# Second block, second mixer: the attention units begin in the column of the sparse keys, and two turns of results move between the tiles of the last query column

## What is computed

```
def odd_mixer(x, w_in, q_norm_g, kv_norm_g, w_uq, w_ukv, w_o):
    qc, kc, vc, qi, ki, wi, cq, ckv, kr = split_cols(x @ w_in, ODD_SIZES)
    out_c = dsa_attention(qc, kc, vc, qi, ki, wi)      # 8 heads, 64 best keys by an index score
    q  = rms_norm_2(cq, q_norm_g) @ w_uq               # 8 heads of 64 + 32 (rotated)
    kv = rms_norm_2(ckv, kv_norm_g) @ w_ukv            # 8 heads of 64 keys + 64 values
    out_d = causal_block_attention(q, k, v)            # k: kv's keys and the shared rotated kr
    return concatenate([out_c, out_d], axis=-1) @ w_o
```

## Time and profile before

| what | us |
|---|---|
| median of 3 timed runs | 2582.02 |
| lowest and highest of them | 2581.15, 2609.4 |
| the profiled execution, its own time | 2592.51 |
| its span, first to last instruction | 2590.7 |
| busy in the span: PE, DVE, ACT | 2452.1, 1719.2, 1194.5 |
| mean granted PE clock | 0.953 of full speed |

### The profile page before, as it was taken

How to read it: one execution, slowest core, us unless ns; L and a number is a source line. 1 busy time by engine, 2 the same in 40 slices (tenths; PEclk the granted TensorE clock), 3 DMA queues, 4 the chain that set the end, 5 groups by cost and what they waited for, 6 DMA issues and landing times.

```text
span 2590.7 us, 34009 instructions
## 1 busy us (share of the span) xinstructions
PE 2452.1 (95%) x14244; PEld 2102.6 (81%) x14244; DVE 1719.2 (66%) x2263; ACT 1194.5 (46%) x1520; POOL 98.7 (4%) x187
## 2 busy tenths in 40 slices
PE   5999999899999999999999998989999899899998
PEld 1788888767789999998899997867777787778776
DVE  5897776652656656655556655568878775688786
ACT  3222212333434444445444444456656644566665
POOL 0111111010000000000000000000000000000000
PEclk8999999998869999999899998999999896999999
DMA  6677887322114554455334452238877630388774
GB/s 257 216 243 255 267 265 260 131 76 95 66 35 161 179 195 163 175 193 217 139 131 164 178 203 99 82 128 332 333 270 297 252 114 33 114 330 321 287 301 181
DMA packets 80387, 501.19 MB, mean 193 GB/s; under 512 B 9604, under 2 KB 10708, under 8 KB 28496
## 3 DMA queue, kind: packets, MB, share of 16 engines
q1 hardware_dynamic: 59120, 423.66, 44.4%
q0 software_dynamic: 21088, 75.01, 9.1%
HBM read 497.58 MB, written 1.05 MB: 192 GB/s over the span
## 4 chain that ended last, share of the span: by engine, by line
PE 69%; DVE 16%; ACT 9%; issue 3%; DMA 2%; DVEq 0%; ACTq 0%; SPq 0%; POOL 0%; POOLq 0%
PE bank L394 67%; DVE wl L1913 7%; ACT wh L1304 6%; DVE macc L1949 2%; ACT s L1394 1%; DVE f L2074 1%; PE bank L577 1%; DMA raw<-in_wstream 1%; DVE s L2065 1%; DMA raw<-in_wmod 1%; PE bank L1198 1%; DVE rs L1973 1%; DVE hl L2049 1%; ACT H L1403 0%; DVE tmp L2042 0%
## 5 line engine op out<-in xcount | busy, mean ns | idle before, releaser
L1913 DVE TENSOR_TENSOR wl<-raw,wh 128x2048 fp32r<-128x2048 f32 (+1 forms) x430 | 903.8, 2107 | 404.7 <-ACT wh L1304 402.1
L1304 ACT ACTIVATE wh<-raw 128x2048 fp32r<-128x2048 f32 (+1 forms) x430 | 755.0, 1763 | 366.4 <-PE bank L394 354.3
L394 PE MATMUL bank<-hh,wh 128*128 128x258 f32 (+2 forms) x2200 | 700.8, 319 | 43.9 <-DVE wl L1913 23.5
L394 PE MATMUL bank<-hh,wl 128*128 128x258 f32 (+2 forms) x2200 | 681.5, 310 | 0.0
L394 PE MATMUL bank<-hl,wh 128*128 128x258 f32 (+2 forms) x2200 | 680.1, 309 | 0.0
L394 PEld LDWEIGHTS bank<-hh,wh 128*128 128x128 f32 x2200 | 428.1, 195 | 72.3 <-issue 23.0
L394 PEld LDWEIGHTS bank<-hl,wh 128*128 128x128 f32 x2200 | 429.0, 195 | 18.5
L394 PEld LDWEIGHTS bank<-hh,wl 128*128 128x128 f32 x2200 | 427.4, 194 | 19.2
L394 PE MATMUL bank<-wh,hh 128*128 128x512 f32 (+1 forms) x704 | 278.4, 395 | 5.5 <-DVE hl L2825 2.8
L394 PE MATMUL bank<-wl,hh 128*128 128x512 f32 (+1 forms) x704 | 274.0, 389 | 0.0
L394 PE MATMUL bank<-wh,hl 128*128 128x512 f32 (+1 forms) x704 | 274.0, 389 | 0.0
(11 more groups left out here) (424 smaller groups left out, 2716.8 us busy)
## 6 DMA issues: line engine op xcount, KB each, us to landing
raw<-in_wstream SPq DMA_DIRECT2D x393, 1024.0 KB, 5.0
mring<-in_wmod POOLq DMA_DIRECT2D x128, 512.0 KB, 4.6
raw<-in_wmod SPq DMA_DIRECT2D x8, 1024.0 KB, 9.1
X<-in_xT SPq DMA_DIRECT2D x1, 2048.0 KB, 12.3
bias<-in_nabias POOLq DMA_DIRECT2D x16, 128.0 KB, 2.5
c_sglg<-in_sglg POOLq DMA_DIRECT2D x1, 1024.0 KB, 5.2
c_sglb<-in_sglb POOLq DMA_DIRECT2D x1, 1024.0 KB, 7.5
out<-X SPq DMA_DIRECT2D x4, 256.0 KB, 2.2
```

Of the source, the lines that this page charges most:

```text
L394: return e.matmul(out, lhsT, rhs, start=start, stop=stop, skip_group_check=True)
L1304: e.activation(wh[i % NB][:, o], raw[i % NR][:, o], ACT.Copy).then_inc(*slab_high(st.split + m))
L1913: e.tensor_tensor(wl[i % NB][:, o], raw[i % NR][:, o], wh[i % NB][:, o].bitcast(F32), ALU.subtract).then_inc(*slab_low(st.split + m))
```

## The change

The column okc moves from before the latent projections to behind them, and five unit steps go into it, each followed by a selection step. The oqc columns 1 and 2 have six unit steps each where there were five, and column 3 has five. Its turns 2 and 3 stand behind its tiles 5 and 6. So all 22 steps that came before the output projection are now between tiles, and `attend(5)` and the loop of turns and units are gone. `middle` becomes a table from tile to function. ACT copies both turns out, does unit 21 and only then copies out the last oqc column. DVE makes both low parts and then does unit 21. The projection's own 14 steps are as before. Four selection steps of okc are gone, and a later step stands between units for each.

```diff
--- before.py
+++ after.py
@@ -981,7 +980,7 @@
                 ins.then_inc(*result("ossq"))
 
 
-            def p(chunks, c0, key, m0=0, pumps=False, units=(), middle=None):
+            def p(chunks, c0, key, m0=0, pumps=False, units=(), middle={}):
                 for m in range(m0, m0 + chunks):
                     b = bank((key, m), act_out, key, m)
                     st.kept.add(bank_of[key, m])
@@ -993,13 +992,13 @@
                         if k in units:
                             attend(1)
                             pump(1)
-                        if k == 3 and middle:
-                            middle()
+                        if k in middle:
+                            middle[k]()
                     st.kept.remove(bank_of[key, m])
 
             p(2, 8, "ocq")
             p(1, 10, "ock")
-            p(1, 7, "oki", middle=root_sum)
+            p(1, 7, "oki", middle={3: root_sum})
             p(2, 5, "oqi")
             project_tok("oin", 12, P, 2, h, dve_out, "ovw")
             st.selection = selection()
@@ -1012,8 +1011,7 @@
                 w.wait_ge(const_in["oswap"], 0)
                 mm(b[:, 0:n * T].rearrange("p (h t) -> p h t", h=n), od.osw[:], src, True, True).then_inc(*result(*key))
 
-            p(1, 0, "oqc", pumps=True, middle=lambda: rotate(("rot", "kr"), od.kr[:].unsqueeze(1), act_out, "okr", 0))
-            p(1, 4, "okc", pumps=True)
+            p(1, 0, "oqc", pumps=True, middle={3: lambda: rotate(("rot", "kr"), od.kr[:].unsqueeze(1), act_out, "okr", 0)})
 
             def q_part(m):
                 b = bank(("uq", m), act_out, "uq", m)
@@ -1068,14 +1066,15 @@
 
             st.kept.update(range(5))
             st.units = attention("od", OD, od.a, logits, values, (4,))
-            p(3, 0, "oqc", m0=1, units=OD_UNITS)
+            def turn_in(i):
+                turned(i, bank(("turn", "od", i), dve_out, "turn l", "od", i))
+
+            p(1, 4, "okc", units=(1, 2, 4, 5, 7))
+            p(2, 0, "oqc", m0=1, units=(0, 2, 3, 4, 6, 7))
+            p(1, 0, "oqc", m0=3, units=(0, 1, 2, 4, 7), middle={5: lambda: turn_in(2), 6: lambda: turn_in(3)})
             result.mark("h read", "oin")
             pump(100)
             pad()
-            attend(5)
-            for i in (2, 3):
-                turned(i, bank(("turn", "od", i), dve_out, "turn l", "od", i))
-                attend(1)
             out_banks("wo1")
             for d in range(6):
                 for k in (4, 6):
@@ -1750,8 +1749,6 @@
             st.selection = selection()
             p(1, "okr", lambda m: od.kr[:], pumps=True)
             p(1, "oqc", query, 0.125, pumps=True)
-            p(1, "okc", lambda m: od.kc[:], pumps=True)
-
             def q_part(m):
                 taken(2)
                 w.wait_ge(result, "uq", m)
@@ -1772,19 +1769,22 @@
             for q in range(2):
                 e.activation(od.vD[:, q, :], banks[bank_of["ovd", q]][:], ACT.Copy).then_inc(*act_out("ovd", q))
             st.units = attention("od", OD, od.a)
-            p(3, "oqc", query, 0.125, m0=1, units=(2, 3))
-            pump(100)
-            pad()
-            attend(5)
 
             def turned(i):
                 w.wait_ge(result, "turn", "od", i)
                 e.activation(hh[:, 2 * i:2 * i + 2, T:2 * T], banks[bank_of["turn", "od", i]][:].rearrange("p (c t) -> p c t", c=2),
                              ACT.Copy).then_inc(*act_out("turn h", "od", i))
 
-            for i in (2, 3):
-                turned(i)
+            def turns():
+                for i in (2, 3):
+                    turned(i)
                 attend(1)
+                pump(100)
+
+            p(1, "okc", lambda m: od.kc[:], units=(2, 3))
+            p(2, "oqc", query, 0.125, m0=1, units=(3, 3))
+            p(1, "oqc", query, 0.125, m0=3, units=(3, 1), middle=turns)
+            pad()
             for _ in range(14):
                 attend(1)
                 taken(2)
@@ -2678,8 +2678,6 @@
             pump(2)
             rotate(("rot", "kr"), od.kr[:].unsqueeze(1))
             pump(2)
-            taken(KC)
-            pump(4)
             for m in (4, 5, 0, 1, 2, 3):
                 taken(2)
                 if m == 1:
@@ -2703,23 +2701,21 @@
                 e.scalar_tensor_tensor(b[:, 0:n], od.dd[:, qb, 0:n], slope, b[:, 0:n], ALU.mult, ALU.add).then_inc(*dve_out("od biased", u))
 
             st.units = attention("od", OD, od.a, logits, lambda g: heads_of(od.Y, g % 2, 512 if g < 2 else 0))
-            for n in 3 * (2, 3):
+            def turned(i):
+                w.wait_ge(act_out, "turn h", "od", i)
+                e.tensor_tensor(hl[:, 2 * i:2 * i + 2, T:2 * T], banks[bank_of["turn", "od", i]][:].rearrange("p (c t) -> p c t", c=2),
+                                hh[:, 2 * i:2 * i + 2, T:2 * T].bitcast(F32), ALU.subtract).then_inc(*dve_out("turn l", "od", i))
+
+            for n in (2, 3, 3, 3, 3, 3, 3, 1):
                 for _ in range(n):
                     attend(1)
                     pump(1)
                 taken(4)
+            for i in (2, 3):
+                turned(i)
+            attend(1)
             pump(100)
             pad()
-            attend(5)
-
-            def turned(i):
-                w.wait_ge(act_out, "turn h", "od", i)
-                e.tensor_tensor(hl[:, 2 * i:2 * i + 2, T:2 * T], banks[bank_of["turn", "od", i]][:].rearrange("p (c t) -> p c t", c=2),
-                                hh[:, 2 * i:2 * i + 2, T:2 * T].bitcast(F32), ALU.subtract).then_inc(*dve_out("turn l", "od", i))
-
-            for i in (2, 3):
-                turned(i)
-                attend(1)
             for _ in range(14):
                 attend(1)
                 taken(2)
```

More of the change, by code:

```diff
@@ L93 @@
 SELECTION_STEPS = 14
-OD_UNITS = (1, 2, 4, 5, 7)
 W1 = T + 2
```

## The result

| what | before | after |
|---|---|---|
| median of timed runs, us | 2582.02 (17 runs) | 2614.6 (17 runs) |
| lowest and highest | 2574.23, 2620.47 | 2585.95, 2626.01 |
| the profiled execution, its own time | 2592.51 | 2626.01 |
| its span | 2590.7 | 2624.2 |
| mean granted PE clock | 0.953 | 0.939 |

The ratio of after to before is 1.0098, with a 95% interval of 1.0067 to 1.0129. It is the ratio of the means without the slow runs (one of before's and two of after's): 2612.2 against 2586.8 us, 25.4 us apart, where the medians are 32.6 apart, since before's runs spread upwards. The change costs about 1% (17 to 33 us by the interval). That lies within the 2% of the forecast's chances, but it is clear of no change. The profiled execution of after is the highest of its 17 runs.

A forecast was written before the change was run, and what follows sets the result against it. TensorE, busy 95% of the span, and its clock bound the kernel. From 2115.9, 72.6 us at 0.50 plus a 1.2 us wait reach 2189.7 against 2161.61: +28 on 2582.0, forecast 2610 us; own range 2600 to 2617, wider range 2576 to 2618.

The forecast's parts named there:

- PE ends the value projection at 2109: Before okc: moving okc's tiles and four score matmuls away ends PE's value projection at about 2109, not 2115.0.
- DVE gains only a split, PE is freed at 2115.9 after 1.8 us: Start of okc: DVE saves one 0.60 us split; PE waits 1.8 us for unit 0's exponential, to 2115.9.
- The clock falls between 2113 and 2118: Inside okc: too few wide tile matmuls, 0 to 2 in 4 us, drop the clock to 0.50; forecast case 0.73.
- It would not come back soon: Columns after the fall: at 0.50 tile matmuls are thinner, 2.5 to 3.8 per 4 us, so the clock stays down.
- The price, 72.6 us of PE work up to the projection: From 2115.9 to the output projection: PE's tiles, logits, transposes, products and turns at 0.50 take 72.6 us, to 2188.5.
- All waits counted: Attention columns: PE's waits taken as 1.8 us for unit 0's exponential and 1.2 before the projection; turns add none.
- The wait before the projection, 1.2 us with bounds of 0.42 and 2.2: Before the projection's first tile: PE waits 1.2 us for ACT's last query-column copy, behind both turns and unit 21's exponential.
- The projection's length unchanged: Output projection: runs at 0.50 in both kernels, so its length stays and what follows shifts whole.
- DVE: first bias at 2114 to 2115, long waits for PE in the columns: DVE in the columns: first bias at 2114 to 2115, then long waits for PE where it now has almost none.
- Rival 2: Columns and output projection: the clock holds through both, projection's units 15 us shorter, 2565 us; chance 0.05.
- rival 3: The clock falls in okc but recovers at the turns, projection at 1.00: +13 us, 2595 us; chance 0.08.
- The two rules of the Trainium skill: Columns: idle gaps drop the clock, so fuller columns keep it, 2580 us; transposes don't count as busy, so the forecast stands.

The follow-up runs named there:

- okc_units_only: Against the changed kernel: okc keeps its move and five units, but the other columns and turns stand as before the change; ratio to before 1.011, 2616.3 us.
- turns_only: Against the changed kernel: okc stays before the latent projections; all 22 steps and both turns in the three oqc columns; ratio to before 1.0122, 2616.64 us.
- fill_after: Changed kernel plus 37 unread matmuls on 128 rows, in the columns' unit steps and before the output projection; ratio to before 1.007, 2607.61 us.
- okc_dense: Against the kernel before: okc moved behind the latent projections without units in it, all else as before; ratio 0.9981, 2583.73 us.
- fill_after_more: Changed kernel plus 68 unread wide matmuls, in unit steps, between okc and the next column, and around the projection's start; ratio to before 0.9964, 2579.13 us.
- fill_after_32rows: Changed kernel plus 37 unread matmuls on 32 of the 128 rows, in unit steps and before the projection; ratio to before 1.0169, 2636.13 us.

## Why the prediction was right, point by point

The forecast was 2610 us, by a fall of the clock inside okc with no recovery, worth 28 us. Measured were 2614.6, and that mechanism.

- *PE ends the value projection at 2109.* Its last matmul starts at 2108.93. Held.
- *DVE gains only a split, PE is freed at 2115.9 after 1.8 us.* It was freed at 2115.73 after 1.37 us. Held.
- *The clock falls between 2113 and 2118.* At 2117.40. Held, but the ground given doesn't bear it, and in that the hit is in part luck. 0 to 2 matmuls with a tile's high part as weights were expected in the last 4 us; before the fall there were 4, as in before's thinnest stretch of the columns, where the clock held. In okc_units_only there were 5, with PE busy throughout, and in turns_only 8. Before's own trace had such a case that the prediction left out, a fall to 0.50 right behind this stretch, in which PE was busy 4.00 of 4.00 us:

```profile
1624.94:1628.94 4.00, 0.90 (x6) 1.00 0.00 0
```

  So the count doesn't tell where the clock falls. What the runs show is that it fell in okc in the traces of the four kernels that have units there and no more added matmuls than fill_after, and not in okc_dense, where okc has none.
- *It would not come back soon.* It didn't, up to the last units, but for 3.41 us behind the turns, across the wait before the projection.
- *The price, 72.6 us of PE work up to the projection.* From 2115.73 to the end of the last row before the projection's wait, at 2189.81, there are 74.1 us, with the wait of 1.47 in them: 72.6 of work. Errors cancel in this. Single tiles take 0.91 us (2144.24 to 2145.15), not 0.78, while a turn took 0.70 and not 0.96 (2185.64 to 2186.34), and the first 1.7 us ran at the full clock.
- *All waits counted.* This step was incomplete. okc's bank is one of the three that rotate, and score matmuls of the same column take the other two. So oqc column 1 claims okc's own bank for its first tile, and must wait for ACT's copy, which now stands behind unit 4's exponential and a split. The order showed it; only the last column's copy was looked at. It cost 1.47 us.
- *The wait before the projection, 1.2 us with bounds of 0.42 and 2.2.* 1.47. Together the three differences (-0.17, +1.47, +0.27) give the projection's start at 2191.28 and not 2189.7.
- *The projection's length unchanged.* From its first tile to the last transposes 37.8 us now, 38.1 before (2161.61 to 2199.74). Held; the profile's other 4 us lie later. There the stretch from 2431 to the end has a mean granted clock of 0.96, the one from 2400 in before 0.98. No run tells whether the change has a part in that, and before's own runs differ by 46 us.
- *DVE: first bias at 2114 to 2115, long waits for PE in the columns.* 2114.38, and 15.6 us in one group alone.

The median is 4.6 us above the forecast, of which the missed wait and the size of the other explain 1.7. Rival 2 (the clock holds, in the projection too) is what fill_after_more made by force; rival 3 (a recovery at the turns) showed for 3.41 us and didn't last; the wait for o_qc and the projection's units followed, and no run tells which of them ended it.

The two rules of the Trainium skill that were weighed came out as follows. The row of fill_after_32rows, 94.11 us busy of 95.57 at clock 0.50, speaks once more against idle time as the only cause; idle gaps are the cause that the page TensorE: Matmul & The Clock Gate (section Why this matters for your kernels) names. A fall behind a wait of 1.4 to 1.8 us, as in after and fill_after, agrees with it in direction; the one in okc_units_only, ahead of the wait, doesn't. The same page says in Part 4: PE-mode transpose that transposes don't count as busy in the same way. The runs don't settle this: with the turns between tiles the clock rose right behind them, at 2189.08 in after and at 2203.43 in fill_after_32rows, and fell again 3.41 us later, and no run took the transposes by themselves.

What stays open: what sets the moment of the fall, and why a part of before's own runs is as slow as most of after's (2608.01, 2609.4, 2620.47). An early fall would explain them, but no profile of such a run is there. Within before's runs beside the experiments the time goes with the mean granted clock: 2561.08 us at 0.966, 2601.54 at 0.948.

## What to carry to other kernels

Where PE is at 95% busy, look at the granted clock of each stretch before you look at waits: filling the gaps of a column with narrow work (matmuls on 64 or 32 rows, transposes) can slow down everything in it. Keep narrow work between enough wide tiles; how many are enough, no run here tells. Where they can't be had, try a few wide matmuls that nobody reads: here they cost less than they gave back when they held the clock to the end (26 of them gained 0.5%, 37 that held it for a part gained nothing certain). When a column moves, list the bank that the next column claims and who empties it.

## What the runs showed of the hardware that was not expected

- Of two kernels that differ only in whether 37 added matmuls use 128 or 32 rows, the second is 28.5 us slower, with PE busy 94.11 of 95.57 us at 0.50.
- The low clock lasts: at 0.50 the tiles spread out, PE has few gaps (busy 112.71 of 116.06 us), and it stayed there for all of these in okc_units_only, through columns of five units such as ran at 1.00 in before. It ended with the units: at 2225.91 there, at 2230.04 in after. That the slower pace itself keeps the clock down fits this, but isn't shown.
- The moment of the fall varies: 4.1, 4.7, 5.2 and 8.2 us behind okc's first tile in fill_after_32rows, okc_units_only, fill_after and after.
- Half the change cost as much as the whole (1.011 and 1.0122 against 1.0098): the price depends on when the clock falls, not on how much was moved.
- Added work made both orders faster: 0.9938 for before with 25 added matmuls, and 35 us off after with 68.
